# A two-model layer kernel on one core: when ScalarE exponentiates, where the softplus runs, and the banks of the last merge

## What is computed

```python
# first block, latent attention, per head and block of 128 queries: causal softmax over all earlier keys
p = softmax(mask((q_nope @ k_nope.T + q_rope @ k_rope.T) * 192 ** -0.5)); o = p @ v
# second block
score = where(causal, sum_h(relu(q_idx[h] @ k_idx.T) * w_idx[h]), -inf)      # 8 index heads of 64
_, sel = top_k(score, min(256, s // 4))                                      # 128 keys of each query
dt = softplus(dt_raw + dt_bias); a = -exp(a_log)                             # 32 heads, time steps of the state space
y = gated_group_rmsnorm(ssd_scan(...), z, ssm_norm)                          # 4 groups of 512 channels
merged = sigmoid(g_att) * y_att + sigmoid(g_ssm) * (y @ w_ssm_out)
x = x + merged @ w_out
```

## Time and profile before

| | |
|---|---|
| runs, median (lowest to highest) | 2642.8 us (2638.73 to 2652.48), 3 runs |
| the profiled execution | 2640.71 us, span 2638.5 us |
| mean granted clock of TensorE | 0.99 |
| PE busy | 2543.2 us, 96% of the span |
| DVE, POOL, ACT busy | 1537.7, 1135.6, 669.7 us (58%, 43%, 25%) |
| HBM | 165 GB/s over the span |
| chain that ended last | PE 49%, POOL 18%, issue 18%, DVE 10%, ACT 2% |

### The profile page before, as it was taken

The page is one execution under the profiler, slowest core; times in us unless marked ns, Lnnn a source line. Parts: engine busy times, 40 slices in busy tenths (PEclk is TensorE's granted clock), DMA queues, the critical chain, the costliest instruction groups (busy, mean ns, idle before and its releaser), DMA issues.

```text
span 2638.5 us, 30948 instructions
## 1 busy us (share of the span) xinstructions
PE 2543.2 (96%) x11668; PEld 2025.1 (77%) x11668; DVE 1537.7 (58%) x2061; ACT 669.7 (25%) x1317; POOL 1135.6 (43%) x765
## 2 busy tenths in 40 slices
PE   8999999999989999999999999999999998999998
PEld 6888888888767778888887777777776666888886
DVE  5764665464775534645657684434446898677721
ACT  2002520021344421201113213333322442222200
POOL 4333455555521225555554443333332224555554
PEclk9999999999989999999999999999999999999999
DMA  6434465555532236555655474454454535555664
GB/s 207 128 108 132 156 191 195 195 191 196 176 96 64 72 104 192 191 192 191 208 192 165 162 210 158 157 162 153 144 183 161 171 116 168 191 193 194 192 196 167
DMA packets 149560, 436.61 MB, mean 165 GB/s; under 512 B 14064, under 2 KB 18352, under 8 KB 149424
## 3 DMA queue, kind: packets, MB, share of 16 engines
q1 hardware_dynamic: 64480, 200.29, 25.4%
q0 software_dynamic: 67840, 201.35, 21.9%
q10 hardware_dynamic: 17104, 33.14, 3.7%
HBM read 417.90 MB, written 16.83 MB: 165 GB/s over the span
## 4 chain that ended last, share of the span: by engine, by line
PE 49%; POOL 18%; issue 18%; DVE 10%; DVEq 2%; ACT 2%; DMA 0%; POOLq 0%; ACTq 0%; SPq 0%
POOL w_lo L424 15%; PE bank L481 12%; PE bank L483 11%; PE bank L484 11%; POOL w_hi L396 4%; PE bank L952 2%; PE bank L1129 1%; PE bank L1120 1%; DVE dsa_work L2273 1%; PE bank L686 1%; DVE rope_sum L2109 1%; PE bank L939 1%; DVE mla_probs L2408 1%; PE bank L1155 1%; DVE ssm_y L2439 1%
## 5 line engine op out<-in xcount | busy, mean ns | idle before, releaser
L424 POOL TENSOR_TENSOR w_lo<-w_raw,w_hi 128x1024 fp32r<-128x1024 f32 x375 | 900.2, 2401 | 11.9 <-DMA w_hi<-stream 3.8
L396 POOL DMA_DIRECT2D w_hi<-stream x376 | 226.7, 603 | 1473.3 <-PE bank L481 1284.5
L481 PE MATMUL bank<-x_hi,w_hi 128*128 128x512 f32 x1464 | 587.1, 401 | 18.5 <-POOL w_lo L410 12.0
L483 PE MATMUL bank<-x_lo,w_hi 128*128 128x512 f32 x1464 | 572.5, 391 | 0.0
L484 PE MATMUL bank<-x_hi,w_lo 128*128 128x512 f32 x1464 | 572.5, 391 | 0.0
L481 PEld LDWEIGHTS bank<-x_hi,w_hi 128*128 128x128 f32 x1464 | 276.5, 189 | 102.0 <-issue 39.7
L484 PEld LDWEIGHTS bank<-x_hi,w_lo 128*128 128x128 f32 x1464 | 276.2, 189 | 58.7
L483 PEld LDWEIGHTS bank<-x_lo,w_hi 128*128 128x128 f32 x1464 | 276.8, 189 | 56.3 <-issue 2.4
L2056 DVE TENSOR_TENSOR relu_sq<-relu 128x512 f32<-128x512 f32 x64 | 181.2, 2831 | 98.3 <-ACT relu L1428 98.3
L481 PE MATMUL bank<-hidden_hi,w_hi 128*128 128x512 f32 x512 | 199.2, 389 | 0.0
L483 PE MATMUL bank<-hidden_lo,w_hi 128*128 128x512 f32 x512 | 199.2, 389 | 0.0
(11 more groups left out here) (438 smaller groups left out, 4513.4 us busy)
## 6 DMA issues: line engine op xcount, KB each, us to landing
w_hi<-stream POOLq DMA_DIRECT2D x376, 512.0 KB, 4.7
w_raw<-stream SPq DMA_DIRECT2D x376, 512.0 KB, 3.7
projections<-spill_out ACTq DMA_DIRECT2D x56, 256.0 KB, 2.1
ssm_x<-projections ACTq DMA_DIRECT2D x4, 1024.0 KB, 7.5
gate_tiles<-projections ACTq DMA_DIRECT2D x16, 256.0 KB, 3.0
ssm_z<-projections ACTq DMA_DIRECT2D x16, 256.0 KB, 2.7
residual<-x_in SPq DMA_DIRECT2D x4, 512.0 KB, 6.7
toeplitz_hi<-toeplitz_rows_hi POOLq DMA_DIRECT2D x4, 512.0 KB, 6.7
```

Source lines behind the costliest of these rows:

```text
L396: e.dma_start(in_slot(whi, t % SLOTS, o), in_stream(o)).then_inc(hi_ready[t % SLOTS], 16)
L424: e.tensor_tensor(wlo[:, s, :], raw[:, s, :], whi[:, s, :].bitcast(F32), ALU.subtract).then_inc(lo_ready, 1)
L481: mm = e.matmul(out, wh, rh, start=first, stop=False)
L483: e.matmul(out, wh, rl, start=False, stop=False)
```

## The change

Three parts. In latent attention ScalarE makes the copy of item n-3 first and then the exponential of item n-1 (it was: the exponential of item n, then the copy), and VectorE normalises item n-2 (it was n-1). In the index steps VectorE makes the first three instructions of the softplus after step 1 and the rest after step 4, with ScalarE's two exponentials in its step 3; the residual's scalings move one step earlier, and the tile `ssm_a` moves to a free place. In the last merge the units `o`, 3, m use banks 4 to 7 and `ys`, 3 bank 3; VectorE works in the bank itself, ScalarE and VectorE read the bank for the two parts, and unit m waits, from m = 4 on, for the low part of m-4.

```diff
@@ TensorE, state space and sparse block
+        def unit_bank(u):
+            kind, g, j = UNITS[u]
+            if kind == "ys" and g == 3:
+                return bank[3]
+            return bank[4 + j % 4] if (kind, g) == ("o", 3) else bank[6 + u % 2]
...
-                o = bank[6 + u % 2]
+                o = unit_bank(u)
                 a, d = freed_before(u - 1)
-                if by_act(u - 2):
+                if (kind, g) == ("o", 3):
+                    if j >= 4:
+                        e.wait_ge(nx_lo, 8 * T_OUT + j - 3)
+                    elif j >= 2:
+                        e.wait_ge(un_dve, freed_before(UNIT_AT["o", 2, 7] + 1)[1])
+                elif (kind, g) == ("ys", 3):
+                    pass
+                elif by_act(u - 2):
@@ ScalarE, mla
-                    if n < MLA_ITEMS:
-                        w = (n % 4 + 1) * P
-                        e.wait_ge(at_m, n + 1)
-                        if n >= 3:
-                            e.wait_ge(at_t, n - 2)
-                        e.activation(mpr[:, n % 3, 0:w], bank[n % 3][:, 0:w], ACT.Exp, scale=MLA_SCALE,
-                                     bias=mnm[:, n:n + 1], accum_out=mrs[:, n:n + 1]).then_inc(at_e, 1)
                     m = n - MLA_AHEAD
                     if m >= 0:
...
+                    x = n - 1
+                    if 0 <= x < MLA_ITEMS:
+                        w = (x % 4 + 1) * P
+                        e.wait_ge(at_m, x + 1)
+                        if x >= 3:
+                            e.wait_ge(at_t, x - 2)
+                        e.activation(mpr[:, x % 3, 0:w], bank[x % 3][:, 0:w], ACT.Exp, scale=MLA_SCALE,
+                                     bias=mnm[:, x:x + 1], accum_out=mrs[:, x:x + 1]).then_inc(at_e, 1)
@@ ScalarE, projections (the same two lines leave the loop over C_UNITS, n == 1)
+                    if s == 3:
+                        e.wait_ge(dt_dve, 1)
+                        e.activation(sz[:, 2, :], sz[:, 1, :], ACT.Exp)
+                        e.activation(sam[:, :], col("a_log", 0, 32), ACT.Exp).then_inc(dt_act, 1)
@@ ScalarE, state_space (root reads unit_bank(u) too)
-                    e.activation(xh3[:, m, :], acc[:, m, :], ACT.Copy, scale=0.5).then_inc(nx_hi, 1)
+                    e.activation(xh3[:, m, :], bank[4 + m % 4][:, :], ACT.Copy, scale=0.5).then_inc(nx_hi, 1)
@@ VectorE, mla
-                    m = n - 1
+                    m = n - 2
@@ VectorE, projections
                 for s in range(8):
-                    stt(h[:, s, :], h[:, s, :], col("final_norm", s), row1[:, :], ALU.mult, ALU.mult)
+                    for m in ((0, 1), (2,), (3,), (4,), (5,), (6,), (7,), ())[s]:
+                        stt(h[:, m, :], h[:, m, :], col("final_norm", m), row1[:, :], ALU.mult, ALU.mult)
...
                     for n in range(3 * s, 3 * s + 3):
                         index_scores(n)
+                    if s == 1:
+                        time_steps()
+                    if s == 4:
+                        time_steps_rest()
                 e.drain()
-                time_steps()
                 top_keys()
@@ VectorE, state_space
-                        u = UNIT_AT["o", 3, m]
-                        a = acc[:, m, :]
-                        add_scaled(u)
+                        b = bank[4 + m % 4][:, :]
+                        e.wait_ge(un_full, UNIT_AT["o", 3, m] + 1)
+                        if m == 0:
+                            e.wait_ge(y_rstd, 4)
+                        tt(b, b, grs[:, :], ALU.mult)
+                        e.drain()
+                        tt(b, b, acc[:, m, :], ALU.add)
                         e.drain()
                         e.wait_ge(g_loaded[m % 2], 16 * (4 + m // 2) + 16)
-                        stt(a, gates[:, m % 2, :], 1.0, a, ALU.add, ALU.mult)
+                        stt(b, gates[:, m % 2, :], 1.0, b, ALU.add, ALU.mult)
                         e.drain()
-                        tt(a, a, mg[:, m, :], ALU.add).then_inc(nx_gain, 1)
+                        tt(b, b, mg[:, m, :], ALU.add).then_inc(nx_gain, 1)
                     if m:
                         j = m - 1
                         e.wait_ge(nx_hi, 8 * T_OUT + j + 1)
-                        stt(xl3[:, j, :], acc[:, j, :], 0.5, xh3[:, j, :].bitcast(F32), ALU.mult,
+                        stt(xl3[:, j, :], bank[4 + j % 4][:, :], 0.5, xh3[:, j, :].bitcast(F32), ALU.mult,
                             ALU.subtract).then_inc(nx_lo, 1)
```

More of the change, by code:

```diff
@@ L336, in build @@
         sds, scd = at("ssm_decay_states", 196, [P, ST, 32]), at("ssm_chunk_decay", 196.5, [P, ST, 32])
-        nsac, sam = at("ssm_neg_acum", 197, [P, ST, 32]), at("ssm_a", 197.5, [P, 32])
+        nsac, sam = at("ssm_neg_acum", 197, [P, ST, 32]), at("ssm_a", 107, [P, 32])
         sat_rows, both = at("ssm_acum_t", 198, [64, S], F32R), at("hi_and_lo_row", 207.5625, [64, 32], F32R)
@@ L1624, in projections @@
                 for n, x in enumerate(C_UNITS):
[L1625 to L1628, removed]
                     unit(UNIT_AT[x])
@@ L1736, in root @@
                         e.wait_ge(un_dve, freed_before(UNIT_AT["o", g - 1, 7] + 1)[1])
-                    e.activation(grs[:, :], bank[6 + u % 2][:, :], ACT.Ln, scale=0.25 / 512, bias=col("eps")).then_inc(un_act, 1)
+                    e.activation(grs[:, :], unit_bank(u)[:, :], ACT.Ln, scale=0.25 / 512, bias=col("eps")).then_inc(un_act, 1)
                     e.drain()
@@ L2292, in time_steps, with time_steps_rest @@
                 e.drain().then_inc(dt_dve, 1)
+            def time_steps_rest():
                 e.wait_ge(dt_act, 1)
```

## The result

| | before | after |
|---|---|---|
| median (lowest to highest), 7 runs each | 2638.73 us (2637.18 to 2652.48) | 2622.59 us (2619.66 to 2626.8) |
| profiled execution's span | 2638.5 us | 2623.4 us |
| PE busy, mean granted clock | 2543.2 us (96%), 0.99 | 2534.9 us (97%), 0.99 |
| ratio to the kernel before | | 0.9919 (0.9901 to 0.9938) |
| the changed kernel in another group, 6 runs | 2642.65 us, 10 runs | 2618.52 us, 0.9904 (0.9884 to 0.9924) |

The change makes the kernel about 0.8% faster (16 us between the medians, 21 by the ratio, 25 by the ratio of the second group). That is clear of the 0.5% that a measurement tells from no change. The forecast was 2620 us and a gain of 22.9.

The account below looks back on a forecast made before the run. TensorE, at work 96% of the span, was taken as the bound, with its waits and the lower clock behind them. -6.8 - 10.5 - 5.6 = -22.9 us gave 2617.8 profiled, 2620 as median; range 2608 to 2632.

Parts of the forecast that it names:

- Softplus, -10.5: Index steps: both TensorE waits and lower clock behind them go; -10.5 us, bounds -5.2 and -11.
- Rival (d): Index steps: VectorE stays over 10 us behind, selected keys late; -5.2 of that part, 2625; 0.10 with (f).
- Last merge, -5.6: Last merge: no VectorE instruction held, `w_out` product starts earlier; -5.6 us, bounds 0 and -7.
- Rival (f): Last merge: the bank change does nothing, ScalarE and VectorE hold each other off; 2625.5; 0.10 with (d).
- Latent attention, -6.8: Latent attention: waits for ScalarE's copies go at three rotations, later normalising costs in heads without units; -6.8 us net.
- rival (a): Latent attention gives nothing, new waits for the normalised items eat it; 2627; 0.20 with (c).
- the second place behind a rotation: Latent attention, two steps on: item 10 normalised behind second rotation and low parts; 1.0 us of new wait.
- The first place: Latent attention, at a rotation: transposes wait 1.7 us for normalised item 7, next scores start 4.15 us earlier.
- the rotations and the steps between them: Latent attention: net 3.1 us won at each of three rotations, -9.3 us; from both sides -14 and -4.5.
- the tail: Latent attention, last heads, without units: later normalising makes transposes wait; +2.5 us, bounds 0 and +5.
- Rival (c): Latent attention: lower clock follows the new waits too, 1.4 us each; part 0, time 2626; 0.20 with (a).
- Rival (e): Latent attention: all 16 heads wait, +37 instead of -6.8; 2664; slower past 1.8 us a head; 0.09.

Follow-up runs that it names:

- `rest_last`: The changed kernel with the long part of the softplus after step 7 instead of step 4; 2623.8 us, 0.9931.
- `c_sbuf`: The changed kernel with four banks kept in the last merge, but VectorE adding into and working in the SBUF tile `acc`; 2626.5 us, 0.9934.
- `lag_again`: Second run of the changed kernel with ScalarE's exponential of item n-1 ahead of the copy of item n-3; 2618.82 us.

## Why the prediction was right, and where its terms were off

The time (2620 forecast, 2622.6 measured, 2618.5 in the second group) and all three signs were right. That the time is within 3 us has luck in it. The forecast subtracted 22.9 us from 2642.8, the median of three runs; the seven runs of the result have 2638.73, 4.1 lower, and the gain between their medians was 16.1, 6.8 smaller; the two differences nearly cancel. By the ratios (21 and 25 us) the gain itself was forecast well. The terms:

- **Softplus, -10.5: measured -11.7** (means of three; -10.4 between the two profiles of the first comparison). Step by step as forecast: both waits gone, `top_keys` ended at 1558.4 inside the forecast 1554 to 1564, and the small matmuls with the unit behind them run at 2.4 GHz. Rival (d), a VectorE that does not catch up, is what `rest_last` shows. (In the working, 1572.94 is the start of the last instruction of `top_keys`; it ended at 1573.17, 0.97 us before TensorE went on and not 1.2, which changes no term.)
- **Last merge, -5.6: measured -6.2** (-5.8 in the pair). grs ended at 2183.63 + 0.63 = 2184.26 and the first product with `w_out` began at 2204.35, 20.1 us behind it where 20 was forecast and 25.9 it was. No instruction was held. Rival (f) was tested by `c_sbuf`: the banks alone cost time. Source in a bank or in SBUF: 0.69 to 0.70 us for 512 columns both ways, so the estimate of -4.8 by the Trainium skill ("VectorE: DVE Perf Modes", The TRN2 errata) was the worse one: its 120 + N cycles for a PSUM source against 58 + N are not seen here.
- **Latent attention, -6.8: measured -4.4**, between the forecast and the 0 of rival (a). The term that was too small is the second place behind a rotation ("two steps on ... 1.0 us of new wait"). The first place was right: 1.7 us of new wait forecast, 1.64 measured at the first rotation (0.97 at the others), the next scores 4.6 us earlier where 4.15 was forecast. But the second place has two waits, 0.75 and 1.57, the latter with a hold by GpSimd's subtraction in it, and cost 2.7 us where 1.0 was forecast. So the new waits of a rotation are 3.3 to 4.0 us, as long as the old one of 3.51, and what is left as gain is the clock. In the pair of profiles the rotations and the steps between them gave -8.1 instead of -9.3, the first head -0.4 instead of 0, and the tail cost +3.6 instead of +2.5; in `lag_again`, which had no lower clock there, the tail cost nothing (-0.3). From one head to the next at the end it was 9.3 us, where 8.8 was to become 9.7.
- **Rival (c)**, the clock that follows the new waits, came true at the tail (6.8 us of lower clock from 950.0 on, where there was none before, one of the signs named for being wrong) and not at the rotations. The forecast had charged the clock by a single figure of 1.4 to 1.5 us for a wait, from one profile, where the same wait was followed by anything from none to 13.7 us of it.
- **Rival (e)**, waits in every head with units, did not come: the 14 waits of L973 are 2 in the first head, 3 at each rotation and 3 at the end, none elsewhere. Its threshold was mis-summed: by its own numbers the whole turns slower past 16.1 / 16 = 1.0 us a head, not 1.8.

## What to carry to other kernels

When an in-order engine stalls, list everything queued behind the stalled instruction before moving one piece out from behind it: moving the copy alone moved the 3.5 us to the next copy in the queue; making the blocking instruction itself one step later cleared them all. Where TensorE is nearly full, a few short waits can cost less than one long wait of the same sum, so compare granted clocks as well as waits, and never from a single profile. Where GpSimd subtracts beside it, a two-input instruction of VectorE should have an input in a PSUM bank, or stand where being late costs nothing.

## What the runs showed of the hardware

- **Which waits the lower clock came with.** Over the 13 profiles, a stretch at 1.2 GHz began within the wait or up to 4.5 us behind it for waits of TensorE of 2.5 us up to 4 in 48 of 51 cases, of 2.0 to 2.5 us in 21 of 34, of 1.0 to 2.0 in 23 of 210, of 0.7 to 1.0 in 6 of 261 (some of the shorter ones only stood beside a long one). The one of 11 to 12 us at the very start never had it. The Trainium skill ("TensorE: Matmul & The Clock Gate", What's actually happening) has the clock fall when the array is idle; these runs agree in kind, and show how seldom a wait under 2 us did it here.
- **How long the clock stays low is not fixed by the code**: 0, 3.4, 10.2 and 13.7 us at the place of the 2.9 us wait shown above.
- **Holds.** An instruction of VectorE with two SBUF inputs that began within 0.25 us of the start of a subtraction of GpSimd ended about 0.6 us behind its end in the cases above (2.91, 3.12 and 3.17 us for 0.68 to 0.69). With a bank among its inputs it was never held: 0.70 us eight times out of eight in the last merge. The scaling of the probabilities, with one SBUF input and a column of factors, was held as well (1.56 for 0.42). The Trainium skill ("SBUF — State Buffer", Who interferes with whom) describes both: two SBUF inputs contend with a GpSimd instruction that reads SBUF, and `tensor_scalar` can enter a mode that does. The trace agrees with it.
